# Gates of the third branch before its output units, convolution taps on one engine

## What is computed

```python
h = rms_norm(x, ln1_g)
z = h @ w_in
z_a, z_b, z_c, z_g = jnp.split(z, split_at, axis=-1)

u, v = jnp.split(gelu(z_a), 2, axis=-1)              # branch A
v = layer_norm(v, sg_ln_g, sg_ln_b)
y_a = (u * chunked_spatial_gating(v, sg_w, sg_b)) @ w_a_out

p, g_lin = jnp.split(z_b, 2, axis=-1)                # branch B
c = p * sigmoid(g_lin)
c = causal_depthwise_conv(c, cv_w, cv_b)             # 31 taps, 512 channels
c = silu(layer_norm(c, cv_ln_g, cv_ln_b))
y_b = c @ w_b_out

q, k, vv = jnp.split(z_c, 3, axis=-1)                # branch C
y_c = stick_breaking_attention(rms(q), rms(k), vv) @ w_c_out

gates = sigmoid(z_g.reshape(bsz, t, 3, d) + b_gate)
merged = gates[0] * y_a + gates[1] * y_b + gates[2] * y_c
x = x + merged @ w_out
```

## Time and profile before

| what | value |
|---|---|
| median of three timed runs | 1332.16 us (1332.08 to 1332.62) |
| the profiled execution | 1334.19 us |
| its span, first to last instruction | 1332.4 us |
| mean granted TensorE clock | 0.994 of 2.4 GHz |
| PE, PEld busy | 1300.1, 1045.6 us |
| DVE, ACT, POOL busy | 855.3, 627.1, 135.9 us |

### The profile page before, as it was taken

How to read it: one execution, slowest core, us unless ns; L and a number is a source line. 1 busy time by engine, 2 the same in 40 slices (tenths; PEclk the granted TensorE clock), 3 DMA queues, 4 the chain that set the end, 5 groups by cost and what they waited for, 6 DMA issues and landing times.

```text
span 1332.4 us, 15705 instructions
## 1 busy us (share of the span) xinstructions
PE 1300.1 (98%) x5991; PEld 1045.6 (78%) x5991; DVE 855.3 (64%) x1079; ACT 627.1 (47%) x917; POOL 135.9 (10%) x100
## 2 busy tenths in 40 slices
PE   7999999988999999999999999999999999999997
PEld 6887777776788888888888888887877777778886
DVE  5458789999767676666666334535278878454534
ACT  6234467443343443333343223412378999544232
POOL 0000223453000210000000001200012220000000
PEclk9999999999899999999999999999999999999999
DMA  7431111222322222222333221522311231224211
GB/s 244 175 103 64 63 64 64 88 102 80 110 95 95 95 95 94 94 94 95 97 101 116 96 94 63 189 95 79 111 64 64 81 94 63 93 67 158 95 64 64
DMA packets 98284, 128.74 MB, mean 97 GB/s; under 512 B 2953, under 2 KB 80689, under 8 KB 97713
## 3 DMA queue, kind: packets, MB, share of 16 engines
q1 hardware_dynamic: 98208, 127.93, 28.7%
q10 hardware_dynamic: 16, 0.00, 0.0%
HBM read 121.63 MB, written 6.29 MB: 96 GB/s over the span
## 4 chain that ended last, share of the span: by engine, by line
PE 83%; DVE 12%; ACT 2%; issue 1%; DMA 1%; SPq 0%; ACTq 0%; DVEq 0%
PE PS L1681 81%; DVE CACC L1195 5%; PE PS L1748 3%; DVE WL L1041 2%; ACT WH L586 1%; DMA STAGE<-in_w_in 1%; DVE GS L1292 1%; DVE QK L1143 0%; DVE BL L1318 0%; DVE MERG L1305 0%; DVE XL L1077 0%; DVE XG L1069 0%; DMA LNR<-in_ln_g 0%; DVE MERG L1309 0%; DVE TMPY L1305 0%
## 5 line engine op out<-in xcount | busy, mean ns | idle before, releaser
L586 ACT ACTIVATE WH<-STAGE 128x1024 fp32r<-128x1024 f32 x214 | 225.5, 1056 | 447.5 <-PE PS L1681 428.6
L1041 DVE TENSOR_TENSOR WL<-STAGE,WH 128x1024 fp32r<-128x1024 f32 x214 | 277.7, 1300 | 219.0 <-ACT WH L586 218.6
L1681 PE MATMUL PS<-XH,WH 128*128 128x512 f32 x960 | 384.3, 400 | 6.7 <-DVE WL L1041 6.7
L1681 PE MATMUL PS<-XH,WL 128*128 128x512 f32 x960 | 375.5, 391 | 0.0
L1681 PE MATMUL PS<-XL,WH 128*128 128x512 f32 x960 | 375.5, 391 | 0.0
L1681 PEld LDWEIGHTS PS<-XH,WH 128*128 128x128 f32 x960 | 181.5, 189 | 50.5 <-issue 12.7
L1681 PEld LDWEIGHTS PS<-XL,WH 128*128 128x128 f32 x960 | 181.7, 189 | 38.8 <-issue 2.4
L1681 PEld LDWEIGHTS PS<-XH,WL 128*128 128x128 f32 x960 | 181.3, 189 | 38.8
L1195 DVE SCALAR_TENSOR_TENSOR CACC<-CPAD,VEC,CACC 128x512 f32<-128x512 f32 x90 | 91.8, 1069 | 0.3
L1681 PE MATMUL PS<-WH,XH 128*128 128x512 f32 x224 | 88.0, 393 | 2.3 <-DVE XL L1077 2.3
L1681 PE MATMUL PS<-WH,XL 128*128 128x512 f32 x224 | 87.2, 389 | 0.0
(11 more groups left out here) (295 smaller groups left out, 1912.2 us busy)
## 6 DMA issues: line engine op xcount, KB each, us to landing
STAGE<-in_w_in SPq DMA_DIRECT2D x52, 1024.0 KB, 5.0
STAGE<-in_w_up SPq DMA_DIRECT2D x22, 1024.0 KB, 5.1
STAGE<-in_w_down SPq DMA_DIRECT2D x11, 1024.0 KB, 5.0
STAGE<-in_w_out SPq DMA_DIRECT2D x4, 1024.0 KB, 5.0
STAGE<-in_w_rnn_out SPq DMA_DIRECT2D x4, 1024.0 KB, 5.3
STAGE<-in_w_attn_out SPq DMA_DIRECT2D x4, 1024.0 KB, 5.0
STAGE<-in_w_o SPq DMA_DIRECT2D x4, 1024.0 KB, 5.0
XTOK<-in_x SPq DMA_DIRECT2D x4, 512.0 KB, 6.3
```

What stands on the lines that cost most here:

```text
L586: act.activation(ring(WH, n), staged(n), ACT.Copy).then_inc(hi_done, 1)
L1041: dve.tensor_tensor(ring(WL, n), staged(n), ring(WH, n).bitcast(F32), ALU.subtract)\
L1681: return pe.matmul(out_, lhsT, rhs, start=start, stop=stop, skip_group_check=True)
```

## The change

- **Order of the third branch** (branch index 1, the convolution). Its twelve units were 4 gates, 2 outputs, 4 gates, 2 outputs. They become 8 gates, then 4 outputs. The second four gates drain to a new tile GSB (over the former attention tile AT). The last two output units use banks 0 to 3 in place of 4 to 7, and U_D's units use banks 4 to 7 in place of 0 to 3. SP's transfers follow the new order.
- **Taps.** Tile 3 goes to DVE with the others. `taps` is called with 4 in every block of branches 0 and 1, and with 4 in the first gate block of the third. L722 and L523, and the tile CTMP, are gone.
- **Norm chain.** Sum, mean, squares, variance, root, Silu and the parts BH and BL move from the second half of branch 1 to the gate blocks p = 1 to 5 of the third branch. PE runs the first ones-sum after p = 2 and the second after p = 4 (bank 5), and waits for BH and BL ahead of the output units.
- **UU parts.** BH and BL of UU are made in the block r = 1 in place of r = 2.
- **Query copies.** The first four QKT copies move ahead of the root of SMALL in ACT's stream; the other four stay where all eight were.

The core of the diff:

```diff
     if U_C <= n < U_D:
-        return "M" if (n - U_C) % 6 < 4 else "T"
+        if n < U_C + 24:
+            return "M" if (n - U_C) % 6 < 4 else "T"
+        return "M" if n < U_C + 32 else "T"
...
-            for j in range(1, CVK):
-                pool.wait_ge(cp_prod, j + 1)
-                if j > 1:
-                    pool.wait_ge(cp_add, j - 1)
-                pool.tensor_tensor(CACC[:, 3, :], CACC[:, 3, :], CTMP[:, j % 2, :], ALU.add)\
-                    .then_inc(cp_add, 1)
...
+            def qkt_copies(j):
+                for c in range(KW):
+                    act.wait_ge(qkt_t, 4 * j + c + 1)
+                    act.activation(QKT[:, j, c, :], PS[:, (2, 3, 4, 5, 6, 7, 2, 3)[4 * j + c], :],
+                                   ACT.Copy, scale=col(V_QKG + j)).then_inc(qkt_ready, 1)
+
+            act.wait_ge(xscr_out, 16)
+            act.wait_ge(vec_ready, 3)
+            qkt_copies(0)
             act.wait_ge(vg_var, 1)
...
-                        if b < 2 and q == 0 and r == (2, 0)[b]:
+                        if q == 0 and r == (1, 0)[b]:
...
+            for p in range(10):
+                hi(U_C + 24 + p + 4)
+                if p == 5:
+                    for c in range(KW):
+                        act.wait_ge(c_norm, c + 1)
+                        act.activation(CACC[:, c, :], CACC[:, c, :], ACT.Silu,
+                                       scale=col(V_CLG + c), bias=col(V_CLB + c)).then_inc(c_ready, 1)
+                    act.wait_ge(unit_done, U_C + 24)
+                    act.wait_ge(c_ready, KW)
+                    act.activation(BH[:], CACC[:], ACT.Copy).then_inc(bh_ready, 1)
+                if p < 8:
+                    act.wait_ge(drained, DR_C + 32 + p + 1)
+                    gs = (GS, GSB)[p // 4]
+                    act.activation(gs[:, p % 4, :], gs[:, p % 4, :], ACT.Sigmoid,
+                                   bias=col(V_BG + BRANCHES[2] * KD + p)).then_inc(gs_ready, 1)
...
-            tap_order += [(c, j - (12 if c == 2 else 0)) for j in range(12, CVK) for c in (0, 1, 2)]
-            tap_order += [(2, j) for j in range(CVK - 12, CVK)]
+            tap_order += [(c, j + (12 if c < 2 else 0)) for j in range(CVK - 12) for c in range(KW)]
+            tap_order += [(c, j) for j in range(CVK - 12, CVK) for c in (2, 3)]
...
-                        taps((5, 5, 5, 5, 6, 0)[r])
+                        taps(4)
...
+            for p in range(10):
+                dve.wait_ge(unit_done, U_C + 24 + p + 1)
+                if p < 8:
...
+                    dve.tensor_tensor((GS, GSB)[p // 4][:, p % 4, :], PS[:, p % 4, :], RBC[:], ALU.mult)\
+                       .then_inc(drained, 1)
+                lo(U_C + 24 + p + 4)
+                if p == 0:
+                    taps(4)
...
+                if p == 1:
+                    dve.wait_ge(c_tap, KW * CVK)
...
+                    dve.tensor_tensor(TG1[:], TG1[:], TG0[:], ALU.add).then_inc(c_sum, 1)
...
+                if p == 9:
+                    for m in range(4):
+                        dve.wait_ge(gs_ready, 16 + m + 1)
...
+                        dve.tensor_tensor(TMPY[:], PS[:, 4 + m, :], GS[:, m, :], ALU.mult)\
+                           .then_inc(drained, 1)
+                        dve.wait_ge(drained, DR_C + 40 + m + 1)
+                        dve.tensor_tensor(MERG[:, m, :], MERG[:, m, :], TMPY[:], ALU.add)\
+                           .then_inc(merged, 1)
+            for m in range(4):
+                merged_low(m)
...
+            def gates_first():
+
+                for p in range(8):
+                    pe.wait_ge(drained, DR_C + (24 if p < 4 else 28) + p + 1)
+                    cm_unit(U_C + 24 + p, p % 4, XH, XL)
+                    if p == 2:
+                        pe.wait_ge(c_sum, 1)
+                        pe.wait_ge(drained, DR_C + 32)
+                        mm(PS[:, 4, :], ONES[:], TG1[:], True, True).then_inc(c_mean, 1)
+                    if p == 4:
+                        pe.wait_ge(c_ssum, 1)
+                        mm(PS[:, 5, :], ONES[:], TG0[:], True, True).then_inc(c_var, 1)
+                pe.wait_ge(c_cent, KW)
+                pe.wait_ge(c_ve, 1)
+                pe.wait_ge(bh_ready, 3)
+                pe.wait_ge(bl_ready, 3)
+                for u in range(2):
+                    quad_unit(U_C + 32 + u, u, 4, BH, BL, KW)
+                pe.wait_ge(drained, DR_C + 40)
...
-                cm_unit(U_D + m, m % 4, MH, ML, 0, ready if m == 0 else None)
+                cm_unit(U_D + m, 4 + m % 4, MH, ML, 0, ready if m == 0 else None)
```

More of the change, by code:

```diff
@@ L356, in transfers @@
                 yield rows(w_in, 0, 8, c0, 256)
-            for b in BRANCHES:
+            for b in BRANCHES[:2]:
                 for quad in range(2):
@@ L361, in transfers @@
                     yield rows((w_a_out, w_b_out, w_c_out)[b], 0, 4, quad * 512, 512)
+            for h in range(4):
+                yield rows(w_in, 0, 8, IN_GATE + BRANCHES[2] * D + h * 256, 256)
+            for quad in range(2):
+                yield rows((w_a_out, w_b_out, w_c_out)[BRANCHES[2]], 0, 4, quad * 512, 512)
             for m in range(4):
@@ L697, in _ @@
                 if i == 0:
[L698 to L704, removed]
+                    qkt_copies(1)
                 stick_act(i)
@@ L710, in _ @@
                        .then_inc(tg_act, 1)
[L712 to L725, removed]
+            for b in range(2):
                 if b == 0:
@@ L728, in _ @@
                     src = UU
-                elif b == 1:
+                else:
                     act.wait_ge(att_read, 4)
@@ L756, in _ @@
                                .then_inc(gs_ready, 1)
[L757 to L775, removed]
-                            act.activation(MH[:, m, :], MERG[:, m, :], ACT.Copy).then_inc(mh_ready, 1)
+            for p in range(10):
[14 more added lines that the diff above has]
+                if p == 2:
+                    act.wait_ge(bl_ready, 1)
+                    for c in range(KW):
+                        act.wait_ge(c_cent, c + 1)
+                        act.activation(UU[:, c, :], CACC[:, c, :], ACT.Square).then_inc(c_sq, 1)
+                if p == 4:
+                    act.wait_ge(c_ve, 1)
+                    act.activation(TG0[:], TG0[:], ACT.Sqrt).then_inc(c_sd, 1)
@@ L778, in _ @@
+            for m in range(4):
+                act.wait_ge(merged, m + 1)
+                act.activation(MH[:, m, :], MERG[:, m, :], ACT.Copy).then_inc(mh_ready, 1)
             for m in range(4, KD):
@@ L1279, in merged_low @@
                                   ALU.subtract).then_inc(ml_ready, 1)
-            for b in range(3):
+            for b in range(2):
                 for q in range(2):
@@ L1302, in _ @@
                                 dst = MERG[:, mm, :] if b == 0 else TMPY[:]
-                                if b == 2 and mm:
-                                    dve.wait_ge(merged, mm)
                                 dve.tensor_tensor(dst, PS[:, 4 + m, :], GS[:, m, :], ALU.mult)\
@@ L1308, in _ @@
                                     dve.wait_ge(drained, DR_C + 16 * b + 8 * q + 4 + m + 1)
-                                    ins = dve.tensor_tensor(MERG[:, mm, :], MERG[:, mm, :], TMPY[:],
-                                                            ALU.add)
-                                    if b == 2:
-                                        ins.then_inc(merged, 1)
-                                    else:
-                                        link(ins)
-                        if b < 2 and q == 0 and r == (2, 0)[b]:
+                                    link(dve.tensor_tensor(MERG[:, mm, :], MERG[:, mm, :], TMPY[:],
+                                                           ALU.add))
+                        if q == 0 and r == (1, 0)[b]:
                             src = (UU, ATT)[b]
@@ L1341, in _ @@
-                        if b == 1 and q == 1 and r == 4:
-                            dve.wait_ge(c_var, 1)
-                            dve.tensor_scalar(TG0[:], PS[:, 0, :], 1.0 / W, EPS, ALU.mult, ALU.add)\
-                               .then_inc(c_ve, 1)
-                            dve.wait_ge(c_sd, 1)
-                            link(dve.reciprocal(TG0[:], TG0[:]))
-                            for c in range(KW):
-                                dve.tensor_tensor(CACC[:, c, :], CACC[:, c, :], TG0[:], ALU.mult)\
-                                   .then_inc(c_norm, 1)
@@ L1364, in _ @@
                 dve.wait_ge(merged, 4 + m)
-                dve.tensor_tensor(TMPY[:], PS[:, 4 + m, :], GS[:, m, :], ALU.mult).then_inc(drained, 1)
+                dve.tensor_tensor(TMPY[:], PS[:, m, :], GSB[:, m, :], ALU.mult).then_inc(drained, 1)
                 dve.wait_ge(drained, DR_D - 4 + m + 1)
@@ L1377, in _ @@
                 dve.wait_ge(unit_done, U_D + m + 1)
-                dve.tensor_tensor(X1[:, m, :], PS[:, m % 4, :], X1[:, m, :], ALU.add)\
```

(5 more changed lines are left out.)

112 lines of the change are left out of this document (50 added, 62 removed).

## The result

The changed kernel takes 1324.88 us in the median (1323.74 to 1325.5), the kernel before 1332.21: a ratio of 0.9945, 95% interval 0.9934 to 0.9957. That is faster, by 7.3 us. The forecast was 11.1 us less, 1321.1 us, range 1315.0 to 1326.0: the side and the range hold, but a third of the expected gain did not come.

A forecast was written before the change was run, and what follows sets the result against it. TensorE was taken as the bound, busy 1300.1 of 1332.4 us. The parts, 10.4 + 2.05 + 0.75 + 1.3 - 3.5 = 11.0 us, came off the median of 1332.16: 1321.1 us, range 1315.0 to 1326.0.

The forecast's parts named there:

- part 1: All taps on VectorE: the four WL halts and the clock stretch at 295 us go; gain 10.4 us.
- Part 2: BH and BL of UU one unit earlier: PE's wait at 237.65 us goes; gain 2.05 us, lower end 0.
- Part 3: Query copies before VSG root: QKT halt and slow stretch go, 2.1 us wait at U_B+2 comes; gain 0.75 us.
- Part 4: Third branch: new 3.0 us halt at first sum, 1.3 us of low clock back; norm chain cover 1.4 us.
- Part 5: Merge at U_D: four short PE halts for ML; loss 3.5 us, bounds 2 and 5.2 with a slow stretch.
- A: Clock stays up behind the halt at the first sum: 1.7 us less, 1319.4 us; chance 0.20.
- B: Second and third slow stretch, at the sum, U_D or U_B+2: 1322.4 to 1325.8 us; chance 0.22.
- C: VectorE's 1.175 us per tap after 213 us is the tap's own, not the neighbour's doing: 1345 us; chance 0.04.
- D: Norm chain late, BL ready after T+48.4: each 1 us late costs 1, with 3 us 1324; chance 0.07.
- E: Halts for WL stay because a lone heavy unit sets them: 1329 to 1332 us; chance 0.05.

The follow-up runs named there:

- tile 3 on GpSimd: Changed kernel with tile 3's products on ScalarE and adds on GpSimd again, over 24 blocks, three taps a block on VectorE: 1321.05 us, ratio 0.9923.
- late WL: Changed kernel with WL of unit U_D+1 moved on VectorE behind the last low part ML: 1321.49 us, ratio 0.9914.
- filled halt: Changed kernel with twelve more matmuls into unread bank 7 ahead of the wait for the first sum: 1323.0 us, ratio 0.9925.
- the taps in the old order: Kernel before with tile 3's taps on VectorE, no adds on GpSimd, all else in the old order: 1322.22 us, ratio 0.993.
- the taps ahead: Changed kernel with 5, 5, 5, 5, 5, 0 taps in a half's six blocks, none in the third branch's first gate block: 1320.34 us, ratio 0.9901.

## Why the prediction was right or wrong

**What bounds the kernel, and part 1: right.** L1195's successor keeps its pitch of 0.665 us (four taps in 2.74), GpSimd's adds cost VectorE some 1.0 us each, WL is never late. VectorE ended block r = 5 at T + 11.0, as forecast (T is 344.69; the next drain starts at 355.71). What the forecast did not see is that taking the adds away and spreading the taps each suffice for this gain.

**Part 2: right in size** (PE's first output unit starts at 235.75 with no wait), but mostly by another road: at least 1.4 of the 2.0 us come with the adds on GpSimd that are gone.

**Part 3: mechanism right, but its 0.75 us hung on one slow stretch.** Load, root (1.4 us later, 1.3 said), halt at U_B+2 (2.43, said 2.1) came as worked out. Without a slow stretch behind that halt PE's score matmuls start at 129.31 to 129.45 us (tile 3 on GpSimd, late WL, filled halt), as the forecast had it; with one, in the three traces of the changed kernel, at 130.17 to 130.28. But the 130.00 of before held the slow stretch behind QKT. Its second trace, without it, has

```profile
128.63 0.92 PE L1681 MATMUL PS<-QKT 64*128 64x384 f32 x4
```

So at equal clock the move costs 0.7 to 0.8 us. The forecast's own terms without the 1.7 us of clock behind QKT, 0.75 - 1.7, give a loss of 0.95. The drain of 1.38 us that the Trainium skill gives (ScalarE: Activation LUTs, "What ACT_TABLE_LOAD costs") does not show behind the load at 112.77: the root starts at 114.07.

**Part 4: the halt right, its clock right in all three traces.** First sum forecast at T + 19.3 = 364.0, measured 364.01; halt 2.84 for 3.0; one stretch of 3.4 us. No wait for the second sum. BL ended at T + 49.0, not 47.0, as the slow stretch delayed the chain too, and PE wanted it at T + 50.0: the cover was 1.0 us.

**Part 5: right.** Three halts (0.81, 1.00, 0.99) and not four. U_D takes 9.11 us (416.47 to 425.58) where 5.44 are needed, a loss of 3.7 against 3.5; the forecast's own end times, T + 79.3 and 75.6, are 3.7 apart. The slow stretch that the upper bound allowed for came in one of three traces.

**The step that failed is the term for the clock in the sum: 4.7 us said, about 0.6 measured.** Taken apart, the 11.0 us held 6.3 us of halts and 4.7 of clock: 1.7 behind QKT, 1.7 behind WL and 1.3 net at the sum. PE's last matmul starts at 1325.38 and 1321.91 us in the two traces before and at 1314.79, 1315.35 and 1317.74 after. With the time lost at half clock (the table above) taken off it stands at 1318.5 twice before and at 1311.4, 1311.9 and 1310.9 after (mean 1311.4): the halts gave 7.1 us, against 6.3 said. The clock gave 0.6 us by these traces and nothing by the mean clocks, against 4.7. Both are rough, since half the length of a stretch is the most that it costs: the one at U_D in the third trace is 6.8 us long and delays what follows by 2.4. The forecast read each stretch of one trace as belonging to its halt. Run again, two of the three places of before were at full clock behind equal halts. The QKT halt of 1.9 us had a stretch in two of the four traces that hold it (not in the second trace before and not with the taps in the old order). The new halt at 122.9 had a stretch in all three traces of the changed kernel, and none in three of the four other traces that hold the same halt of 2.4 us (tile 3 on GpSimd, late WL, filled halt; with the taps ahead it had one). The halt of 2.8 us at the first sum had one in all six. A halt buys a chance of a slow stretch, and the change swapped three places with such halts for three others.

**The base was the same slip seen from the other side.** The sum was made from a trace of 1334.19 us and taken off a median of 1332.16, though the text gave both numbers. That trace had lost 6.8 us to the clock and the next one 3.4; a median execution need not have every stretch whose return was counted. Taken off the profiled execution, 1334.19 - 11.0 = 1323.2 us, the sum misses the profiled execution of the changed kernel (1323.74) by 0.5. That is in part luck: it was the fastest of its four.

**Rivals.** A (clock up behind the sum) is refuted by the changed kernel's traces, all three low, B is what the third of them shows (1326.7 us for its execution, beyond B's own 1325.8), C is refuted by the taps in the old order. D and E did not come.

## What to carry to other kernels

Price halts and the clock apart: halts from one trace were right to 0.8 us, the slow stretches differ from execution to execution and want several traces, or an expected value. When a block of work is late for one consumer, first ask what stands between its last input and it: eight taps that could go anywhere cost 2.8 us of halt, and one WL with its wait 2.0 of 3.7. And an early copy ahead of a function from another table set moves the table load as well; give the load its own place.

## What was not expected of the hardware

The spread of the kernel before, 1330.7 to 1335.6 us in 42 executions of one program, seems to come largely with the granted clock: its two traces, 3.5 us apart, differ by 3.4 us of lost clock, and with no halt over 1.0 us left between 110 and 440 us the spread was 0.33 us in four executions. Behind a halt of 1.91 us among the QK transposes the clock fell in one trace of the kernel before and not in the other; behind 3.0 us at the first sum likewise; behind 3.4 us at WL both times, once for 3.4 us and once for 6.8. Which of these happens was not settled; the only run that acted on it is the one with the halt filled.
